# Expert rows dealt over partitions, a gates' product in two column groups, and its weights asked for later, in one decoder step

## What is computed

```python
for e in range(N_EXPERTS):                       # 32
    act = jax.nn.silu(h @ w_gate[e]) * (h @ w_up[e])
    y = y + gates[:, e:e + 1] * (act @ w_down[e])
```

## Time and profile before

| | us |
|---|---|
| median of 3 runs | 693.38 |
| profiled execution | 703.3 |
| its span, first to last instruction | 701.5 |
| TensorE busy | 611.1 (87%) |
| VectorE busy | 279.6 (40%) |
| ScalarE busy | 139.2 (20%) |
| GpSimd busy | 116.4 (17%) |
| mean DMA rate | 230 GB/s |
| mean granted TensorE clock | 0.944 of full speed |

### The profile page before, as it was taken

How to read it: one execution, slowest core, us unless ns; L and a number is a source line. 1 busy time by engine, 2 the same in 40 slices (tenths; PEclk the granted TensorE clock), 3 DMA queues, 4 the chain that set the end, 5 groups by cost and what they waited for, 6 DMA issues and landing times.

```text
span 701.5 us, 8557 instructions
## 1 busy us (share of the span) xinstructions
PE 611.1 (87%) x3155; PEld 328.6 (47%) x3155; DVE 279.6 (40%) x615; ACT 139.2 (20%) x405; POOL 116.4 (17%) x195
## 2 busy tenths in 40 slices
PE   4999999899898999999989996999999777999700
PEld 2444344445544555555545482555555443555300
DVE  3320068333333452568788778311212111121146
ACT  3111041233323454401131000110101100101111
POOL 2350016110040110101021201011121110211023
PEclk9999999999999999999999966999999998999965
DMA  9643337823030210041084798899999999999674
GB/s 282 197 142 135 121 102 207 280 83 118 4 106 15 73 48 0 1 121 62 1 327 156 238 407 328 359 419 419 419 420 421 419 422 421 420 420 415 250 262 166
DMA packets 49378, 161.45 MB, mean 230 GB/s; under 512 B 16443, under 2 KB 17772, under 8 KB 36664
## 3 DMA queue, kind: packets, MB, share of 16 engines
q1 hardware_dynamic: 39624, 143.67, 52.8%
q0 software_dynamic: 7488, 17.19, 7.4%
q10 hardware_dynamic: 2224, 0.04, 0.2%
HBM read 150.91 MB, written 19.01 MB: 242 GB/s over the span
## 4 chain that ended last, share of the span: by engine, by line
PE 68%; DMA 12%; SPq 7%; DVE 5%; ACT 3%; issue 2%; another core or an unknown queue 2%; POOL 1%; POOLq 0%; DVEq 0%; ACTq 0%
PE bank L1869 11%; PE bank L1872 11%; PE bank L2090 8%; PE bank_p L2140 6%; PE scores L2153 6%; DMA WS<-in_w_down_e 4%; DMA FT<-in_w_down_e 4%; PE bank_t L2140 4%; PE bank_t L1886 3%; SPq L552 3%; SPq L555 2%; DMA WS<-in_w_in 2%; SPq L549 2%; PE bank L2132 2%
## 5 line engine op out<-in xcount | busy, mean ns | idle before, releaser
L1872 PE MATMUL bank<-WS,XHT 128*128 128x512 f32 x192 | 87.4, 601 | 2.0 <-DMA WS<-in_w_in 1.5
L1869 PE MATMUL bank<-XHT,WS 128*128 128x512 f32 x192 | 85.0, 597 | 1.0 <-PE bank_t L1886 1.0
L1869 PEld LDWEIGHTS bank<-XHT,WS 128*128 128x128 f32 x192 | 35.7, 190 | 43.3 <-issue 43.0
L1872 PEld LDWEIGHTS bank<-WS,XHT 128*128 128x128 f32 x192 | 34.8, 190 | 42.5 <-issue 40.4
L2140 PE MATMUL bank_p<-WS,XHT 128*64 128x256 f32 x288 | 45.5, 391 | 5.7 <-DVE XHT L1724 1.5
L915 POOL DMA_INDIRECT out_rows<-MVA,slot_ids x17 | 17.0, 1001 | 188.1 <-DVE MVA L1741 188.1
L2140 PE MATMUL bank_t<-WS,XHT 128*64 128x256 f32 x288 | 43.0, 381 | 1.5 <-DMA FT<-in_w_up_e 0.8
L2140 PEld LDWEIGHTS bank_p<-WS,XHT 128*64 128x64 f32 x288 | 27.7, 141 | 21.0 <-issue 4.3
L1741 DVE COPY MVA<-scores 128x512 f32<-128x512 f32 x17 | 11.8, 692 | 56.9 <-PE scores L2153 56.9
L806 POOL TENSOR_SCALAR rr<-ss 128x1 f32<-128x1 f32 (+3 forms) x25 | 7.9, 316 | 158.7 <-ACT XHT L1145 46.3
L2140 PEld LDWEIGHTS bank_t<-WS,XHT 128*64 128x64 f32 x288 | 26.3, 137 | 15.6 <-DMA FT<-in_w_up_e 1.2
(11 more groups left out here) (427 smaller groups left out, 1022.6 us busy)
## 6 DMA issues: line engine op xcount, KB each, us to landing
WS<-in_w_gate_e SPq DMA_DIRECT2D x16, 1024.0 KB
WS<-in_w_up_e SPq DMA_DIRECT2D x16, 1024.0 KB
WS<-in_w_down_e SPq DMA_DIRECT2D x16, 1024.0 KB
WS<-in_w_in SPq DMA_DIRECT2D x6, 2048.0 KB, 11.8
XHT<-in_w_gate_e SPq DMA_DIRECT2D x10, 1024.0 KB
XHT<-in_w_up_e SPq DMA_DIRECT2D x10, 1024.0 KB
XHT<-in_w_down_e SPq DMA_DIRECT2D x10, 1024.0 KB
FT<-in_w_gate_e SPq DMA_DIRECT2D x6, 1024.0 KB
```

The lines of the kernel that those rows point to most:

```text
L1869: mm = pe.matmul(PS[r][:, :], w[:, k, 128 * m:128 * (m + 1)], hT[:, k, 0:512], start=(k == 0), stop=(k == KC - 1))
L1872: mm = pe.matmul(PS[r][:, :], hT[:, k, 128 * m:128 * (m + 1)], w[:, k, :], start=(k == 0), stop=(k == KC - 1))
```

## The change

- `riota`, against which the place in a pair is compared, is filled in another order: the 32 places of a half expert go first to the partitions 0, 4, 8, ... 28 of their 32, then to 1, 5, ..., and so on. Gathers and stores use the same `slot_ids`.
- The gates' product of the 512 prompt columns is made as two products of 256 columns for each k, at partitions 0 and 64 of bank t. ScalarE then has six activations in place of four.
- ScalarE issues the two loads of `wg` before its copy of tile 1 of dq, no more at the start.
- The first slots: the constants 64 x expert - 4096 and pair start - 4096 are made once, at the first logits, and three small operations in `rank` become one.
- The twelve operations behind the table of pairs become `pair_places()`, called after `rows_of(0)`.
- `rows_in` signals after each half, and `gate_up` waits for one half before k = 0 and for the other before k = 4.

```diff
@@ constants (GpSimd) @@
-            link(pool.iota(iscr[:, :], [[1, 128]], base=0, channel_multiplier=0))
+            link(pool.iota(iscr[:, :], [[32, 4], [1, 8], [8, 4]], base=0, channel_multiplier=0))
             link(pool.tensor_copy(riota[:, :], iscr[:, :]))
@@ ScalarE: start, gates, acc @@
-            g = w_in[0].rearrange("(p k) n -> p k n", k=KC)[:, :, W_COLS["gates"]:W_COLS["gates"] + 8]
-            act.wait_ge(wg_zeroed, 1)
-            act.dma_start(wg[:, :, 0:H], g[:, :, 0:H]).then_inc(wg_in, 16)
-            act.dma_start(wg[:, :, 32:32 + H], g[:, :, H:2 * H]).then_inc(wg_in, 16)
...
-                    act.activation(rI[:, N4:TOK], PS["t"][0:H, :], ACT.Identity, bias=bgi[:, :])
+                    for u in range(2):
+                        act.activation(rI[:, N4 + 256 * u:N4 + 256 * u + 256], PS["t"][64 * u:64 * u + H, 0:256],
+                                       ACT.Identity, bias=bgi[:, :])
...
-                    act.activation(rF[:, N4:TOK], PS["t"][32:32 + H, :], ACT.Identity, bias=bgf[:, :]).then_inc(freed["t"], 1)
+                    act.activation(rF[:, N4:N4 + 256], PS["t"][32:32 + H, 0:256], ACT.Identity, bias=bgf[:, :])
+                    act.activation(rF[:, N4 + 256:TOK], PS["t"][96:96 + H, 0:256], ACT.Identity, bias=bgf[:, :])\
+                        .then_inc(freed["t"], 1)
...
                     b, m = item[1:]
+                    if (b, m) == ("dq", 1):
+                        g = w_in[0].rearrange("(p k) n -> p k n", k=KC)[:, :, W_COLS["gates"]:W_COLS["gates"] + 8]
+                        act.wait_ge(wg_zeroed, 1)
+                        act.dma_start(wg[:, :, 0:H], g[:, :, 0:H]).then_inc(wg_in, 16)
+                        act.dma_start(wg[:, :, 32:32 + H], g[:, :, H:2 * H]).then_inc(wg_in, 16)
@@ VectorE: logit 0, rank, order @@
+                        v.tensor_scalar(early_rows[:, :], eidx[:, 0:2 * EARLY], float(SLOTS), float(-NOROOM), ALU.mult, ALU.add)
+                        link(v.tensor_scalar(early_pairs[:, :], piota[:, 0:EARLY], float(-NOROOM), None, ALU.add))
...
-                    link(v.scalar_tensor_tensor(early, eidx[:, None, 0:ne].to_broadcast([128, NTILES, ne]), float(SLOTS), early,
-                                                ALU.mult, ALU.add))
-                    link(v.tensor_scalar(early, early, float(-NOROOM), None, ALU.add))
+                    link(v.tensor_tensor(early, early, early_rows[:, None, :].to_broadcast([128, NTILES, ne]), ALU.add))
...
-                    link(v.tensor_scalar(slot_of, slot_of, float(NOROOM), None, ALU.add))
-                    place_rows(first_onehots, piota[:, 0:EARLY])
+                    place_rows(first_onehots, early_pairs[:, :])
...
-                    link(v.tensor_tensor(xs, xin, rest, ALU.subtract))
...
-                    link(v.scalar_tensor_tensor(d1, d1, float(NEXP + 1), pos, ALU.add, ALU.subtract))
+            def pair_places():
...
+                link(v.tensor_tensor(xs, xin, rest, ALU.subtract))
...
+                link(v.scalar_tensor_tensor(d1, d1, float(NEXP + 1), pos, ALU.add, ALU.subtract))
@@ VectorE: experts @@
-                return ins
...
+                                    ALU.mult).then_inc(xt_evac, 1)
...
-                rows_in(xT[s]).then_inc(xt_evac, 1)
+                rows_in(xT[s])
...
             rows_of(0)
+            pair_places()
             late_ids()
@@ TensorE: gates, experts @@
-                    for b, c0, c1_ in (("t", 0, 512), ("p", 512, TOK)):
-                        for k in range(KC):
-                            mm = pe.matmul(PS[b][0:36, 0:c1_ - c0], wg[:, k, :], hT[:, k, c0:c1_],
+                    for k in range(KC):
+                        for u in range(2):
+                            mm = pe.matmul(PS["t"][64 * u:64 * u + 36, 0:256], wg[:, k, :], hT[:, k, 256 * u:256 * u + 256],
                                            start=(k == 0), stop=(k == KC - 1))
-                        mm.then_inc(filled[b], 1)
+                    mm.then_inc(filled["t"], 1)
+                    for k in range(KC):
+                        mm = pe.matmul(PS["p"][0:36, 0:N4], wg[:, k, :], hT[:, k, 512:TOK], start=(k == 0), stop=(k == KC - 1))
+                    mm.then_inc(filled["p"], 1)
...
-            def gate_up(gu, rows, w, due):
+            def gate_up(gu, rows, w, due, evacuated):
...
+                        if g == 0 and k % 4 == 0:
+                            pe.wait_ge(xt_evac, evacuated + (1 if k else 0))
...
-                    pe.wait_ge(xt_evac, i)
+                    pe.wait_ge(xt_evac, 2 * i)
...
-                pe.wait_ge(xt_evac, i + 1)
...
-                gate_up(PS["t" if s else "p"], xT[s], w, 32 * (n // NSETS) + 32)
+                gate_up(PS["t" if s else "p"], xT[s], w, 32 * (n // NSETS) + 32, 2 * i + 1)
```

More of the change, by code:

```diff
@@ L454, in build @@
         piota = sb("piota", [128, NPAIRS])
+        early_rows, early_pairs = Wd[:, 0, 0:2 * EARLY], Wd[:, 1, 0:EARLY]
         iscr = moflat[:, 0:128].bitcast(i32)
@@ L1676, in _ @@
                     v.nop().then_inc(table_ready, 1)
-                    link(v.tensor_tensor(xs, xin, rest, ALU.subtract))
[L1679 to L1689, removed]
-                    link(v.scalar_tensor_tensor(d1, d1, float(NEXP + 1), pos, ALU.add, ALU.subtract))
+            def pair_places():
+                one32, extra, key, key2, top, incl, below, rest, xin, xs, pos, d1, d2, q, u_ = e32
+                link(v.tensor_tensor(xs, xin, rest, ALU.subtract))
+                link(v.tensor_tensor(q, eidx[:, :], below, ALU.subtract))
+                link(v.tensor_scalar(u_, q, float(2 * FULL), 2.0, ALU.is_ge, ALU.mult))
+                link(v.tensor_tensor(q, q, u_, ALU.add))
+                link(v.scalar_tensor_tensor(pos, below, float(2 * FULL), q, ALU.add, ALU.subtract))
+                link(v.tensor_tensor(pos, pos, top, ALU.mult))
+                link(v.tensor_tensor(pos, pos, q, ALU.add))
+                link(v.scalar_tensor_tensor(u_, xs, 2.0, below, ALU.add, ALU.subtract))
+                link(v.tensor_tensor(u_, u_, top, ALU.mult))
+                link(v.tensor_tensor(d2, u_, top, ALU.subtract))
+                link(v.tensor_tensor(d1, xs, u_, ALU.subtract))
+                link(v.scalar_tensor_tensor(d1, d1, float(NEXP + 1), pos, ALU.add, ALU.subtract))
             def late_ids():
@@ L1723, in rows_in @@
                 for half in range(2):
-                    ins = v.tensor_tensor(dst[:, 4 * half:4 * half + 4, :],
-                                          bank[half][:, :].rearrange("p (k t) -> p k t", t=128),
-                                          gffn[:, 4 * half:4 * half + 4, None].to_broadcast([128, 4, 128]), ALU.mult)
-                return ins
+                    v.tensor_tensor(dst[:, 4 * half:4 * half + 4, :],
+                                    bank[half][:, :].rearrange("p (k t) -> p k t", t=128),
+                                    gffn[:, 4 * half:4 * half + 4, None].to_broadcast([128, 4, 128]),
+                                    ALU.mult).then_inc(xt_evac, 1)
             def rows_of(i):
@@ L1770, in further_pair @@
                 dve.wait_ge(xt_filled, i + STATIC)
-                rows_in(xT[0]).then_inc(xt_evac, 1)
+                rows_in(xT[0])
                 dve.wait_ge(silu_done, i + STATIC)
@@ L2202, in further_pair @@
                 rows_out(XG[0]).then_inc(xt_filled, 1)
-                pe.wait_ge(xt_evac, i + STATIC)
-                gate_up(PS["p"], xT[0], 0, 32 * i + 32 * ((PAIRS + NSETS - 1) // NSETS))
+                gate_up(PS["p"], xT[0], 0, 32 * i + 32 * ((PAIRS + NSETS - 1) // NSETS), 2 * i + 2 * STATIC - 1)
                 pe.wait_ge(act_done, i + STATIC)
```

## The result

| | before | after |
|---|---|---|
| median, us | 696.42 (15 runs) | 689.62 (15 runs, 685.98 to 695.11) |
| ratio, 95% interval | | 0.9905 (0.9884 to 0.9926) |
| span of the profiled execution | 701.5 | 689.0 |
| TensorE busy | 611.1 | 608.1 |
| mean DMA rate, GB/s | 230 | 234 |

The change makes the kernel 0.95% faster, 6.6 us. The forecast was 8.7 us, a ratio of 684.7/693.38 = 0.9875, which lies outside the interval. The forecast time, 684.7, is 4.9 us too low: 3.0 of that is the median of before, which is 696.42 over fifteen runs and was 693.38 over three; the rest is the effect, forecast 2 us too large. One profile can't settle 2 us: single times of one kernel here spread over 9 us, and the two spans differ by 12.5, nearly twice the medians. So I first cut the two spans at the same products of TensorE, to see which stages hold a term and which only scatter.

A forecast was written before the change was run, and what follows sets the result against it. TensorE was taken to bound the kernel until about 400 us, then DMA streaming expert weights. Terms 0.6 + 3.4 + 0.7 + 3.8 + 0.2 = 8.7 us off 693.38 gave 684.7, range 681 to 688.7 plus a microsecond.

The forecast's parts named there:

- Gates' product (-3.4): Gates' product at 81.04 us: two column groups take 3.61 us instead of 7.03, saving 3.4 us.
- rival (2): TensorE's saving is lost before 400 us, at a later wait or by column groups in turn; 688.1 us, chance 0.09.
- From there to 400 us nothing is tied to an absolute time: After the gates' product until 400 us, loads wait only for blocks used, so time saved earlier is kept.
- I let 4.0 us pass through: The savings at the start and the gates' product, 4.0 us, reach 400 us whole.
- Start (-0.6): Kernel start: without the gates' small-piece loads beside it, the first projection weight block lands 0.6 us earlier.
- Rows dealt out (-3.8): End of the experts' weight stream: levelling rows over the DMA engines makes the last engine finish 3.8 us earlier.
- Rival (1): Levelling gives nothing: engines share rows another way or wait for something shared; 688.7 us, chance 0.18.
- Rival (3): The DMA engines that gain rows are slow ones, so levelling gives less; 685.8 or 687.8 us, chance 0.10.
- Routing and first pair (-0.7): Routing gives 0; at the first pair, signals by halves start the product and the weight stream 0.7 us earlier.
- Rival (4): Slower: the gates' weights come late and TensorE waits before their product; 701 us if landing takes 40, chance 0.04.
- Sum: Whole kernel: 0.6 + 3.4 + 0.7 + 3.8 + 0.2 = 8.7 us saved, giving 684.7 us.

The follow-up runs named there:

- e2: Kernel before plus only the gates' product in two column groups, with six ScalarE copies for four; 0.9991 of before.
- e10: Kernel before with unused TensorE work in its four waits, plus the gates' product in two column groups; 0.9958 of before.
- e15: Changed kernel with unused TensorE work in its four waits, but the gates' product as before; 0.9913 of before, 689.16 us.
- e16: Whole changed kernel with unused TensorE work in its four waits, the kernel of e8 run again beside its parts; 0.9869 of before, 687.45 us.
- e8: Changed kernel plus unused TensorE work (identity transposes) in four of its waits; 0.9838 of before, 687.54 us.
- e12: Changed kernel with unused TensorE work in its waits and rows dealt to and fro over the engines; 0.9855 of before, 685.93 us.
- e14: Kernel before with unused TensorE work in its four waits, plus only the later loads of the gates' weights; 0.9996 of before.
- e1: Kernel before plus only the dealing out of an expert's rows over the partitions; 0.9965 of before.
- e6: Changed kernel with the rows' places in their old order; 0.9934 of before, 694.98 us.
- e5: Changed kernel run again, as it is, on one chip beside variants of the row order; 0.9893 of before, 690.76 us.
- e9: Kernel before plus unused TensorE work in its four waits, nothing else changed; 0.9993 of before.
- e13: Kernel before with unused TensorE work in its four waits, plus only the rows dealt out; 0.9919 of before.
- e3: Kernel before plus only the later loads of the gates' weights, moved to tile 1 of dq; 0.9972 of before.
- e7: Changed kernel with the rows' places packed, an order made to be bad for the DMA engines; 1.0075 of before, 704.08 us.
- e4: Kernel before plus only the rest: constants for first slots, `pair_places` later, `rows_in` signals by halves; 1.0042 of before.
- e11: Kernel before with unused TensorE work in its four waits, plus the routing's part (first-slot constants, later places, half signals); 0.9984 of before.

## Why the prediction was right and where it was wrong

**Gates' product (-3.4).** Its size was right to 0.05 us in every trace, so the second form of rival (2), the groups running in turn, is out. What failed is the step behind it, "From there to 400 us nothing is tied to an absolute time" and "I let 4.0 us pass through". Measured in times it is worth 0.6 (e2), 2.4 (e10) and 1.7 us (e15 to e16), each to some 2 us or more either way. The traces show two ways in which it is lost. In e10 1.4 us go at a wait for VectorE. Its cached scores hang on page gathers of the key cache, DMAs with waits of their own, which moved up by less than TensorE did, and the first softmax stands behind them in its queue. That is rival (2), first form; I had given it 0.09, and looked for the loss among TensorE's waits of before, where it couldn't show. In e8, e12 and e16 nothing is lost there, and falls of the granted clock at 170 us and later take 1.6 to 1.7 us each. The sum had no term for the granted clock at all, neither here nor at the first tile and the last products.

**Start (-0.6).** First products came 0.3 us earlier in the mean, with ranges that overlap; e14 shows no gain in time, to 2 us either way. The term was mis-sized by half as far as is known: it took the whole difference between 366 and 400 GB/s as the small pieces' doing. What I had no term for is the clock at the first tile, 0 to 3 us of scatter, in kernels of both kinds.

**Rows dealt out (-3.8).** Right in kind and size. The stream's end moves by 4.3 to 4.5 us in the three pairs of traces that differ in nothing else (before and e1, e6 and e5, e9 and e13), a little over what I took and within the bounds; in times 2.4 (e1), 4.2 (e5 to e6) and 5.1 us (e13 to e9, two chips). A slip in the prediction's count goes the same way: 1072 rows over sixteen engines are 67 in the mean, not 66, which makes the lateness before 8.4 us for 8.8 and the gain 3.8 to 4.4 for 3.4 to 4.2. At the end of the bare kernels 2.8 us arrive (before to e1, up to the end of the trace), for in after, e1 and e5 the last but one down product ran at half pace and took 1.7 us more. The dealing isn't shown to cause that: e3, e6 and e7, which aren't dealt out, have it too, and before, e2 and e4 don't. Rival (1) is out by e6 and e7. Rival (3) is out, since nothing is missing from the 4.4. The Trainium skill, DMA: Bandwidth & Descriptors, section Latency and other measured facts, has engines 7 and 15 as usually slower; no run here shows it.

**Routing and first pair (-0.7).** 0.58 us at the first pair in every unfilled trace with the half signals, 1.0 us in time (e11), with an interval that holds zero. In e4 the 0.58 us didn't reach the end of the stream. The 1.0042 of e4 was not found again, and its lower granted clock is enough to explain it. Rival (4) didn't occur: the weights landed within some 5 us, 20 us before they were needed.

**Sum.** With the terms as measured in bare kernels, and the gates' product as in e15 and e16, 0.3 + 1.7 + 0.6 + 2.8 = 5.4 us (the 2.8 has the end of the kernel in it), beside 6.6 measured; with 4.6, which arrives from e9 to e13, it is 7.2. That 6.6 lies between is in part luck: the 0.3 and the 1.7 are known no better than they are large, and the 0.6 was not seen at the stream's end in e4. The forecast's 8.7 is too large by the part of the gates' product that is lost again (some 1.7), by half the start, and by the half pace of one product. The measured effect lies between the forecast and rival (2), 5.3 us, whose case (the product shorter, the time not) is the one that came, in part.

**Open.** What ScalarE waited for at 121 us in three traces; why e9 gains nothing from the filling while e8 seems to; what makes the granted clock fall in one trace and not in the next, and whether the two column groups have to do with it; and how often the wait of e10 comes.

## What to carry to other kernels

Time saved on the bounding engine passes only if the engines that it meets later are ahead too: read the queue of each at the next meeting point, above all where it waits for a DMA, not the waits of the bound engine. Then set two traces side by side, product by product: a wait shows as one step in the lead (1.4 us in e10), a fall of the granted clock as another (1.6 to 1.7 us), and a step that moves from trace to trace is not the change's own until shown. In a gather of few large rows to many partitions, count the rows per DMA engine; with runs of four partitions 32 apart, dealing them out costs no instruction and here gave 4 us of a 200 us stream. Where single times spread over more than the effect, cut several traces at the same landmarks: stages that repeat to 0.2 us show a term of 0.6 us that no median could.

## What the runs showed of the hardware

- TensorE's granted clock was at 0.50 for 0.67 to 0.96 of the time from 398 to 430 us in every trace, also where TensorE was busy for 9.37 of 10 us. Windows of after:

```profile
400.00:410.00 10.00, 9.37 (x42) 8.47 (x43) 8.59 (x35) 0.00 (x0) 0.00 (x0) 0.50 1.01 408
424.00:429.00 5.00, 5.00 (x26) 3.07 (x26) 4.42 (x19) 0.00 (x0) 0.64 (x1) 0.50 1.01 391
429.00:440.00 11.00, 9.89 (x96) 7.43 (x94) 7.08 (x23) 2.05 (x3) 0.99 (x1) 1.00 0.88 348
```

  The first pair's gate and up products take 9.71 us there, and 7.06 to 7.13 when the clock is up. Twelve unused transposes in the wait before it (e8) brought the transposes of the gathered rows from 1.94 to 1.17 us and the products behind them to 8.7; in e9, with the same twelve, they took 1.97 and 8.8, in e13 1.16 and 10.0. The Trainium skill, TensorE: Matmul & The Clock Gate, Part 1, has the lower clock as the default state, from which activity releases it. The rows agree as to the two levels; in the first of them TensorE is busy for 9.37 of 10 us at the lower one.
- The column of the granted clock can read 1.00 ahead of the first recorded rise (at 19.4 us in after) while the products run at half pace (0.86 us for 0.43 in the first tile); durations are the safer reading at a kernel's start.
- A fall of the granted clock in mid-projection (e16 at 170 us, e12 at 170 and 347 us) put TensorE 1.6 to 1.7 us back each time.
- Waits of 2.4 to 2.6 us before the same down product were followed by full pace in three undealt bare traces (before, e2, e4) and by half pace in three others (e3, e6, e7).
